# Scatters that add scored expert outputs to one total per token, in place of stored rows that are read back

## The chip, the cores and the metric

The kernel runs on one core of one Trainium2 chip. The metric is the device time of one execution in microseconds (us). A core has TensorE (PE in the profile; its weight loads are PEld), VectorE (DVE), ScalarE (ACT), GpSimd (POOL) and SyncE (SP), and 16 DMA engines that move data between the chip's memory and the on-chip SBUF. An engine's own instructions run in order; between engines, and between engines and DMAs, only semaphores hold an order.

## The reference

Two layers over 512 tokens of 1024 features: a Mamba-2 mixer and then a forgetting attention, each followed by a mixture of experts. What the change touches is the mixture of experts, which both layers have:

```python
scores = sigmoid(t @ w_router)                   # 512 x 64
eidx   = top 8 of (scores + bias), inside the 4 best of 8 groups
wsel   = scores at eidx / their sum * 2.5
out = (silu(t @ ws1) * (t @ ws3)) @ ws2          # shared expert
for each expert e:
    a = silu(t @ w1[e]) * (t @ w3[e])
    out += (a * gate[:, e]) @ w2[e]              # gate = wsel where chosen, else 0
x = layer_norm(alpha * x + (1 + gate2) * out)
```

Each token is sent to 8 of 64 experts, so an expert has 64 tokens on the mean (512 * 8 / 64). All is float32.

## The kernel before

All engines' programs are written out by hand, each with its semaphores; nothing is scheduled by a tool. Where several reads stand in one order, that is the order of the code.

**Before the experts.** The mixer's result, normalized, is written as rows to `rows_dram` (512 x 1024). DVE picks each token's 8 experts (`mask`), numbers the tokens of an expert (`pos`), and numbers the experts of a token from 0 to 7 (`krank`, a scan over the mask). PE multiplies a one-hot matrix of the places with `V` (token number times 8, and `krank`), which gives for each of an expert's 128 slots the row `8 * token + rank` that its output will have; a slot without a token gets a number past the end. DVE writes both this number and the token number (shifted by 3) to `table`.

**The expert loop.** 64 experts, in groups of 8 (`SLOTS`), `with ... Fori` over the groups in the middle. For each expert: SP loads w1, w3, w2 (three DMAs of 512 KB) as soon as its slot of eight is free, that is after the `down` product of the expert 8 earlier; POOL (`fetch`) gathers the expert's token rows with an indirect DMA into one of 4 tiles `xg`, five experts ahead; PE transposes them (L771), ACT copies and scales them (L1240), PE makes the two up products (L793), ACT and DVE the gated product, PE the down product (L805); DVE multiplies it with `g2bc` on its way into one of 4 tiles `yrow` (L1829); POOL (`send`, L2173) scatters `yrow` with an indirect DMA to the rows of `part_dram`, a tensor of 4096 rows with one row for each token and rank. Slots without a token have an index out of bounds, and nothing of them is moved. POOL's program is: fetch of expert i + 5, send of expert i, fetch of i + 6, and so on. A `carrier`, a tiny tensor operation (L2148), stands ahead of each indirect DMA and carries its waits. `yrow[u % 4]` may be written again once the scatter of four experts earlier has landed (`y_out`).

**After the loop.** SP reads `part_dram` back by rank: seven DMAs of 2 MB (`rank[k]`, L2428) and the last rank in four of 512 KB (L2432). No rank is complete before the last experts, as each of a token's ranks can be with almost any expert, so load k waits until expert 56 + k is scattered (`until_sent`). DVE multiplies ranks 0 to 2 with the token's gate and adds them to `SH`, which already holds the shared expert and the residual (`add_row`, L1800), partly between the steps of the last group of experts; the gates of each rank are worked out there too (`gates_whole`, `gates_of`, L1778 and L1782). Ranks 3 to 7 go through PE: ACT makes diagonal matrices of gates (`diagonal`, L1255), and PE multiplies each with its rows, 80 matmuls of 128x512 (L875) into all 8 PSUM banks. DVE adds the banks to `SH` (L1934) and normalizes tile by tile. In the first layer the first three weight blocks of the shared keys and values come next on SP; two of their buffers still hold ranks 5 and 6, so they wait for PE (`part_read`).

**Zeros.** Early in the program SP fills `part_dram` with zeros (four DMAs of 4 MB), which makes rows that nothing was scattered to harmless.

An expert with more than 128 tokens takes extra blocks (`more_blocks`, `over`); with these inputs none has, and those branches are not taken.

## Time and profile before

| | us |
|---|---|
| median of 3 runs | 2006.43 |
| lowest, highest | 1999.59, 2013.11 |
| the profiled execution | 2011.6 |
| its span (first to last instruction) | 2009.8 |
| PE busy in the span | 1848.4 (92%) |
| DVE busy | 907.5 (45%) |
| ACT busy | 742.4 (37%) |
| POOL busy | 649.9 (32%) |

The span lies 1.8 us under the profiled execution's time, and that execution 5.2 us above the median. A sum of differences made against the span can therefore be put onto the median unchanged. The page of the profile cuts the span into 40 slices of 50.2 us. The two expert loops lie in slices 14 to 22 and 31 to 40 (about 663 to 1089 us and 1520 to 1950 us). There the row of the DMA engines stands at 8 or 9 tenths and PE at 9.

In the rows below, a line of the timeline reads: start in us, duration in us, engine, line, operation, what it writes and reads, how many, and in brackets the idle time ahead of it with what ended it. SPq is SP's DMA queue: its duration there reaches from the first to the last issue of merged DMAs.

### The profile page before, as it was taken

How to read it: one execution, taken by the hardware profiler on the slowest of the kernel's cores; microseconds unless marked ns; L12 is line 12 of the kernel's file. 1: busy time of each engine (PE TensorE's matmuls, PEld its weight loads, DVE VectorE, ACT ScalarE, POOL GpSimd, SP SyncE). 2: the span in 40 equal slices, each digit the busy share in tenths (PEclk: the TensorE clock that was granted, in tenths of full speed). 3: DMA queues.
4: the chain of work that ended last, by engine and by line, in shares of the span. 5: the costliest groups of instructions: out<-in, count | busy, mean ns of one | idle time of the engine just before them, and what ended most of it. 6: DMA issues, size and time to landing. Idle time of an engine off the chain costs nothing. (4 is left out here: it accounts for less than half of the span.)

```text
span 2009.8 us, 29708 instructions
## 1 busy us (share of the span) xinstructions
PE 1848.4 (92%) x9848; PEld 1275.9 (63%) x9848; DVE 907.5 (45%) x2097; ACT 742.4 (37%) x1913; POOL 649.9 (32%) x796
## 2 busy tenths in 40 slices
PE   2999999988999899999997799999998999999976
PEld 2644444567444688888885346558656888888852
DVE  4677754377313533333345401237444333333453
ACT  2433310255112544444443200134245444444431
POOL 4143300055212474444442340000133744444421
PEclk9799999999999899999998899999998999999988
DMA  9475646491203799999988403200237898999883
GB/s 341 161 273 215 247 151 210 168 335 43 79 11 123 278 334 335 330 328 331 329 293 343 154 28 112 80 17 1 69 112 273 315 328 319 324 342 343 314 313 133
DMA packets 178546, 443.90 MB, mean 221 GB/s; under 512 B 36004, under 2 KB 43540, under 8 KB 178452
## 3 DMA queue, kind: packets, MB, share of 16 engines
q1 hardware_dynamic: 140436, 371.31, 51.6%
q0 software_dynamic: 38016, 71.39, 9.5%
q8 instruction: 53, 0.87, 0.2%
q14 instruction: 41, 0.34, 0.0%
HBM read 419.39 MB, written 90.23 MB: 254 GB/s over the span
## 5 line engine op out<-in xcount | busy, mean ns | idle before, releaser
L1240 ACT ACTIVATE arena<-psum,lncol 128x128 f32<-128x128 f32 x1024 | 371.5, 469 | 423.6 <-PE psum L771 397.4
L793 PE MATMUL psum<-arena 128*128 128x128 f32 x4096 | 501.9, 278 | 0.0
L793 PEld LDWEIGHTS psum<-arena 128*128 128x128 f32 x4096 | 479.2, 193 | 1.0 <-issue 1.0
L805 PE MATMUL psum<-arena 128*128 128x512 f32 x512 | 243.6, 598 | 9.3 <-DVE arena L1829 9.3
L1717 DVE TENSOR_REDUCE destf<-psum 128x3 f32 (+1 forms) x112 | 18.0, 161 | 416.7 <-PE psum L793 399.6
L2148 POOL TENSOR_TENSOR passed<-ones 128x1 f32<-128x1 f32 x256 | 61.1, 239 | 405.2 <-DVE arena L1829 393.8
L557 PE MATMUL psum<-arena 128*128 128x512 f32 x384 | 178.5, 627 | 0.0
L771 PEld LDWEIGHTS psum<-ident,arena 128*128 128x128 f32 x1024 | 123.6, 144 | 74.2 <-issue 65.4
L1829 DVE TENSOR_TENSOR arena<-psum,arena 128x512 f32<-128x512 f32 x256 | 165.7, 683 | 7.8 <-PE psum L805 5.9
L1385 DVE SCALAR_TENSOR_TENSOR arena<-arena,condT 128x512 f32<-128x512 f32 x126 | 150.7, 1196 | 11.7 <-DMA arena<-in_ada_w_dram 7.3
L2164 POOL DMA_INDIRECT arena<-h_rows,idx x128 | 140.5, 1098 | 22.8 <-issue 7.3
L771 PE MATMUL psum<-ident,arena 128*128 128x128 f32 x1024 | 138.5, 280 | 7.1 <-DMA arena<-h_rows,idx 5.0
L2173 POOL DMA_INDIRECT expert_rows<-arena,idx x128 | 131.2, 1025 | 27.2 <-issue 26.9
L2122 POOL DMA_DIRECT2D h_rows<-arena x8 | 4.9, 618 | 416.2 <-ACT arena L1070 416.2
L557 PEld LDWEIGHTS psum<-arena 128*128 128x128 f32 x384 | 76.7, 202 | 94.8 <-issue 94.8
L805 PEld LDWEIGHTS psum<-arena 128*128 128x128 f32 x512 | 88.0, 192 | 73.0 <-issue 71.7
L2073 POOL TENSOR_TENSOR arena<-arena 128x2048 f32<-128x2048 f32 (+1 forms) x20 | 73.1, 3657 | 162.4 <-ACT arena L1097 161.6
L571 PE MATMUL psum<-arena 128*128 128x512 f32 x256 | 111.8, 594 | 0.0
L702 PE MATMUL psum<-arena 128*128 128x512 f32 x256 | 110.9, 592 | 0.0
L1710 DVE TENSOR_TENSOR arena<-slot_no,arena 128x512 bf16<-128x512 bf16 x128 | 87.2, 685 | 0.1
L702 PEld LDWEIGHTS psum<-arena 128*128 128x128 f32 x256 | 48.3, 190 | 58.7 <-issue 58.4
L571 PEld LDWEIGHTS psum<-arena 128*128 128x128 f32 x256 | 48.1, 190 | 57.9 <-issue 57.9
(265 smaller groups left out, 2364.6 us busy)
## 6 DMA issues: line engine op xcount, KB each, us to landing
arena<-in_moe_w_dram SPq DMA_DIRECT2D x384, 512.0 KB
arena<-in_ada_w_dram SPq DMA_DIRECT2D x32, 1024.0 KB, 5.2
arena<-expert_rows SPq DMA_DIRECT2D x14, 2048.0 KB, 13.3
arena<-in_ssm_w_in_dram SPq DMA_DIRECT2D x10, 2048.0 KB, 10.3
arena<-in_ada_w_dram SPq DMA_DIRECT2D x8, 2048.0 KB, 10.8
expert_rows<-arena SPq DMA_DIRECT2D x4, 4096.0 KB, 27.4
arena<-in_ssm_w_out_dram SPq DMA_DIRECT2D x4, 2048.0 KB, 9.4
arena<-in_kv_ada_w_dram SPq DMA_DIRECT2D x4, 1024.0 KB, 5.3
```

What stands on the lines that cost most here:

```text
L557: mm = pe.matmul(ps[:, :], w[:, k, P * j:P * j + P], HT[:, k, :], start=(k == 0), stop=(k == KC - 1))
L571: mm = pe.matmul(ps[:, :], HT[:, k, P * t:P * t + P], w[:, k, :], start=(k == 0), stop=(k == KC - 1))
L702: mm = pe.matmul(ps[:, :], xbcT[:, k, tok(t)], w_blocks[n][k // KC][:, k % KC, :], start=(k == 0), stop=(k == XT - 1))
L771: mm = pe.transpose(psum[:, b, P * j:P * j + P], xg[u % 4][:, P * k:P * k + P], ident[:, :])
L793: mm = pe.matmul(psum[:, b, 0:P], w[:, k, :], xeT[u % 2][:, k, :], start=(k == 0), stop=(k == KC - 1))
L805: mm = pe.matmul(psum[:, b, :], aT[u % 2], exp_w[u][:, 2, 512 * n:512 * n + 512], start=True, stop=True)
L1240: ins = act.activation(xeT[u % 2][:, k, :], psum[:, b, P * j:P * j + P], ACT.Identity, scale=h_scale(l, k), bias=h_shift(l, k))
L1385: ins = dve.scalar_tensor_tensor(ada_acc[0], ada_dve[:, k, :], condT[:, k:k + 1], ada_acc[0], ALU.mult, ALU.add)
L1710: dve.tensor_tensor(onehot[u % 4], slot_no[:, :].unsqueeze(1).to_broadcast([P, T, P]), pos[:, :, one].to_broadcast([P, T, P]), ALU.is_equa ...
L1829: dve.tensor_tensor(yrow[u % YROWS][:, cols_], psum[:, b, :], g2bc[:, cols_], ALU.mult).then_inc(drained[b], 1)
L2164: pool.indirect_dma_start(out=xg[u % 4], out_offset=None, in_=rows_dram, in_offset=bass.IndirectOffsetOnAxis(ap=idx[u][:, 1:2], axis=0), b ...
L2173: pool.indirect_dma_start(out=part_dram, out_offset=bass.IndirectOffsetOnAxis(ap=idx[u][:, 0:1], axis=0), in_=yrow[u % YROWS], in_offset=None,
```

## The change

- `part_dram` (4096 rows, one per token and rank) goes. In its place stands one tensor of 512 rows per layer (`sum_dram[l][a]`, with `SUMS = 1`), one row for each token. Each scatter adds its rows to what is there (`compute_op=ALU.add`).
- Two scatters that add to one row must not overlap in time, so `send` waits until the scatter before it has landed.
- The row index is now the token number itself, so `krank` and the shift by 3 go, and `table` and `idx` have one column.
- The score of a token for its expert has to be with the slot. POOL splits the scores into three bfloat16 parts (`split_scores`), which are columns 2 to 4 of `V`; the one-hot product, now with 5 columns and not 3, brings them to the slots; DVE adds them up (`gslot`), copies one expert's column to `gnow`, and multiplies it into the output in the instruction that empties PSUM. The division by the sum of a token's scores is done at the end with `gsum`.
- After the loop SP reads one total, four tiles of 512 KB, and DVE does one multiply-add per tile (`add_sums`). The eight rank loads, the gates by rank, the diagonals and the 80 matmuls go.
- Zeros are written for two tensors of 2 MB instead of 16 MB.

```diff
-DVE_ROWS = 3
-NOWHERE = 2 * S * TOPK
+SUMS = 1
+NOWHERE = 2 * S
...
-        part_dram = nc.dram_tensor("expert_rows", [S * TOPK, D], F32, kind="Internal").ap()
+        sum_dram = [[nc.dram_tensor(f"expert_sum{l}{a}", [S, D], F32, kind="Internal").ap() for a in range(SUMS)]
+                    for l in range(2)]
...
                             for t in range(T):
-                                pe.matmul(psum[:, b, P:P + 3], onehot[u % 4][:, t, :],
+                                pe.matmul(psum[:, b, P:P + 5], onehot[u % 4][:, t, :],
...
-                for b in range(8):
-                    claim(b)
-                for k in range(DVE_ROWS, TOPK):
-                    pe.wait_ge(gdiag_ready, (TOPK - DVE_ROWS) * l + k - DVE_ROWS + 1)
-                    if k < TOPK - 1:
-                        pe.wait_ge(part_in[k], 16 * (l + 1))
-                    for t in range(T):
-                        if k == TOPK - 1:
-                            pe.wait_ge(last_part_in[t], 16 * (l + 1))
-                        for n in range(2):
-                            mm = pe.matmul(psum[:, 2 * t + n, :], gdiag[T * (k - DVE_ROWS) + t],
-                                           rank[k][:, t, 512 * n:512 * n + 512],
-                                           start=(k == DVE_ROWS), stop=(k == TOPK - 1))
...
                 def write_table(e, ps):
...
+                    dve.tensor_scalar(table[:, one], ps[:, P:P + 1], ps[:, P + 1:P + 2], float(NOWHERE), ALU.add,
+                                             ALU.add).then_inc(table_ready, 1)
+                    return dve.tensor_reduce(gslot[:, one], ps[:, P + 2:P + 5].rearrange("p (e c) -> p e c", c=3), AX, ALU.add)
...
+                    dve.tensor_copy(gnow[:, u:u + 1], gslot[:, one]).then_inc(gate_ready, 1)
...
-                        dve.tensor_tensor(yrow[u % YROWS][:, cols_], psum[:, b, :], g2bc[:, cols_], ALU.mult
-                                          ).then_inc(drained[b], 1)
+                        dve.scalar_tensor_tensor(yrow[u % YROWS][:, cols_], psum[:, b, :], gnow[:, u:u + 1], g2bc[:, cols_],
+                                                 ALU.mult, ALU.mult).then_inc(drained[b], 1)
...
+                def add_sums(a, t):
+                    dve.wait_ge(part_in[a][t], 16 * (l + 1))
+                    return dve.scalar_tensor_tensor(SH[:, t, :], part[a][:, t, :], gsum[:, t:t + 1], SH[:, t, :],
+                                                    ALU.mult, ALU.add)
...
                 for t in range(T):
-                    for n in range(2):
-                        r = SH[:, t, 512 * n:512 * n + 512]
-                        ps = until_filled(dve, ("parts", l, t, n))
-                        dve.tensor_tensor(r, ps, r, ALU.add).then_inc(drained[MARK[("parts", l, t, n)][0]], 1)
...
+                    step(add_sums(SUMS - 1, t))
...
+            def split_scores(l, t0, t1):
+
+                R = slice(t0, t1)
+                pool.wait_ge(sig_ready, T * l + t1)
+                step(pool.tensor_copy(V[:, R, :, 2], scores[:, R, :]))
+                settle()
+                step(pool.tensor_tensor(rest[:, R, :], scores[:, R, :], V[:, R, :, 2], ALU.subtract))
+                settle()
+                step(pool.tensor_copy(V[:, R, :, 3], rest[:, R, :]))
+                settle()
+                pool.tensor_tensor(V[:, R, :, 4], rest[:, R, :], V[:, R, :, 3], ALU.subtract).then_inc(split_ready, 1)
...
                 def send(g, u):
 
                     for b in (3, 7):
                         pool.wait_ge(drained[b], base[b] + SLOTS * g + u + 1)
+                    if u >= SUMS or l or not isinstance(g, int) or g:
+                        v = (u - SUMS) % SLOTS
+                        pool.wait_ge(y_out[v % YROWS], 16 * (2 * g + (v // YROWS + 1 if u >= SUMS else 0))
+                                     + 16 * (E // YROWS) * l)
                     carrier(u)
-                    pool.indirect_dma_start(out=part_dram,
+                    pool.indirect_dma_start(out=sum_dram[l][u % SUMS],
                                             out_offset=bass.IndirectOffsetOnAxis(ap=idx[u][:, 0:1], axis=0),
                                             in_=yrow[u % YROWS], in_offset=None,
-                                            bounds_check=last_part, oob_is_err=False).then_inc(y_out[u % YROWS], 16)
+                                            bounds_check=last_row, oob_is_err=False, compute_op=ALU.add).then_inc(y_out[u % YROWS], 16)
...
-                rows_of = part_dram.rearrange("(t p k) d -> k p t d", p=P, k=TOPK)
-                for k in range(TOPK - 1):
-                    until_sent(sp_, l, E - TOPK + k)
...
-                    sp_.dma_start(rank[k], rows_of[k]).then_inc(part_in[k], 16)
-                when_more(sp_, l, more_blocks, over)
-                until_sent(sp_, l, E - 1)
-                for t in range(T):
-                    sp_.dma_start(rank[TOPK - 1][:, t, :], rows_of[TOPK - 1, :, t, :]).then_inc(last_part_in[t], 16)
+                for a in range(SUMS):
+                    if a == SUMS - 1:
+                        when_more(sp_, l, more_blocks)
+                    until_sent(sp_, l, E - SUMS + a)
                     for t in range(T):
+                        sp_.dma_start(part[a][:, t, :], sum_dram[l][a][TILES[t], :]).then_inc(part_in[a][t], 16)
```

POOL's program inside the loop of the middle groups, before, from one send to the next. `passed` is the carrier's tile; `drained3` and `drained7` say that DVE has emptied the two banks of the down product.

```order
196 L2148 TENSOR_TENSOR passed<-ones 128x1 [waits drained7]
197 L2173 DMA expert_rows<-arena,idx 4096x1024
198 L2157 REGISTER_ALU [waits y_out3]
199 L2158 REGISTER_ALU [waits filled4]
200 L2159 ISA [waits table_ready]
201 L2159 COPY idx<-arena 128x2
202 L2148 TENSOR_TENSOR passed<-ones 128x1 [waits idx_ready]
203 L2164 DMA arena<-h_rows,idx 128x1024
204 L2171 REGISTER_ALU
205 L2171 REGISTER_ALU [waits drained3]
206 L2148 TENSOR_TENSOR passed<-ones 128x1 [waits drained7]
207 L2173 DMA expert_rows<-arena,idx 4096x1024
```

The same place now:

```order
195 L2066 DMA expert_sum<-arena,idx 512x1024
196 L2046 REGISTER_ALU [waits y_out2]
197 L2047 REGISTER_ALU [waits filled4]
198 L2048 ISA [waits table_ready]
199 L2048 COPY idx<-arena 128x1
200 L2037 TENSOR_TENSOR passed<-ones 128x1 [waits idx_ready]
201 L2053 DMA arena<-h_rows,idx 128x1024
202 L2060 REGISTER_ALU
203 L2060 REGISTER_ALU [waits drained3]
204 L2063 ISA [waits drained7]
205 L2037 TENSOR_TENSOR passed<-ones 128x1 [waits y_out0]
206 L2066 DMA expert_sum<-arena,idx 512x1024
```

The instructions and their order are the same; the carrier ahead of the scatter has a further wait, for the landing of the scatter that POOL issued just before (`y_out0` here). The gather of the next expert stands between the two scatters as it did.

SP's program from the last part of the first layer's experts to the weights of the keys and values, before:

```order
199 L2432 DMA arena<-expert_rows 128x1024 [waits y_out2,y_out3,y_out1,y_out0]
200 L2432 DMA arena<-expert_rows 128x1024 x3
201 L2325 DMA arena<-in_ln_g_dram 128x1024
202 L2326 DMA arena<-in_ln_b_dram 128x1024
203 L2302 DMA arena<-in_kv_w_dram 128x8x512
204 L2302 DMA arena<-in_kv_w_dram 128x8x512 [waits part_read]
```

And now:

```order
189 L2309 DMA arena<-expert_sum 128x1024 [waits y_out2,y_out3,y_out1,y_out0]
190 L2309 DMA arena<-expert_sum 128x1024 x3
191 L2218 DMA arena<-in_ln_g_dram 128x1024
192 L2219 DMA arena<-in_ln_b_dram 128x1024
193 L2195 DMA arena<-in_kv_w_dram 128x8x512 x2
```

The seven rank loads ahead of this place are gone, and the second weight block no longer waits for PE to have read a rank.

## Rows read from the trace of the kernel before

**Rows 1.** Stretches inside the two expert loops: each engine's busy time.

```profile
core 0: us, PE busy (x) PEld busy (x) DVE busy (x) ACT busy (x) POOL busy (x), PEclk, DMA share, GB/s
690.00:890.00 200.00, 200.00 (x1512) 167.75 (x1509) 77.88 (x222) 96.10 (x283) 104.39 (x167) 1.00 0.92 329
1560.00:1900.00 340.00, 340.00 (x2570) 285.77 (x2569) 136.01 (x391) 164.90 (x484) 158.70 (x275) 1.00 0.92 330
```

**Rows 2.** Timeline of POOL, two experts of the steady loop.

```profile
746.16 1.01 POOL L2173 DMA_INDIRECT expert_rows<-arena,idx  x1 [0.16 <-issue]
...
747.80 1.05 POOL L2164 DMA_INDIRECT arena<-h_rows,idx  x1
752.22 0.18 POOL L2148 TENSOR_TENSOR passed<-ones 128x1 f32<-128x1 f32 x1 [3.37 <-DVE arena L1829]
752.56 1.02 POOL L2173 DMA_INDIRECT expert_rows<-arena,idx  x1 [0.16 <-issue]
...
758.86 1.01 POOL L2173 DMA_INDIRECT expert_rows<-arena,idx  x1 [0.16 <-issue]
```

**Rows 3.** Timeline at the first layer's loop end: POOL's last nine scatters, in part.

```profile
1044.20 1.02 POOL L2173 DMA_INDIRECT expert_rows<-arena,idx  x1 [0.44 <-issue]
...
1081.28 1.00 POOL L2173 DMA_INDIRECT expert_rows<-arena,idx  x1 [0.15 <-issue]
1085.33 1.09 POOL L2148 TENSOR_TENSOR passed<-ones 128x1 f32<-128x1 f32 x1 [3.05 <-DVE arena L1829]
1086.57 0.99 POOL L2173 DMA_INDIRECT expert_rows<-arena,idx  x1 [0.15 <-issue]
1087.72 1.09 POOL L2148 TENSOR_TENSOR passed<-ones 128x1 f32<-128x1 f32 x1 [0.16 <-DVE arena L1829]
1088.96 1.86 POOL L2173 DMA_INDIRECT expert_rows<-arena,idx  x1 [0.15 <-issue]
```

**Rows 4.** Timeline there: what waited for landings, on ACT and SP.

```profile
1089.40 1.28 ACT L1255 ACTIVATE arena<-ident,gk 128x128 f32<-128x128 f32 x4 [7.31 <-DMA expert_rows<-arena,idx]
...
1093.07 0.36 SPq L2428 DMA_DIRECT2D arena<-expert_rows  x1
1098.71 1.77 SPq L2432 DMA_DIRECT2D arena<-expert_rows  x4
```

**Rows 5.** Timeline at the first loop's start: first gather, first transposes.

```profile
663.48 1.56 POOL L2164 DMA_INDIRECT arena<-h_rows,idx  x1 [0.16 <-issue]
...
671.52 1.97 PE L771 MATMUL psum<-ident,arena 128*128 128x128 f32 x8 [2.56 <-DMA arena<-h_rows,idx]
```

**Rows 6.** Page, part 6: DMA issues, KB each, median us to landing.

```profile
h_rows<-arena POOLq DMA_DIRECT2D x8, 512.0 KB, 3.0
```

**Rows 7.** Page, part 3: DMA queues.

```profile
q1 hardware_dynamic: 140436, 371.31, 51.6%
q0 software_dynamic: 38016, 71.39, 9.5%
```

**Rows 8.** Timeline of SP: when expert weights stop being issued.

```profile
1036.66 2.13 SPq L2375 DMA_DIRECT2D arena<-in_moe_w_dram  x2
1038.88 1.78 SPq L2378 DMA_DIRECT2D arena<-in_moe_w_dram  x1
1051.22 42.21 SPq L2428 DMA_DIRECT2D arena<-expert_rows  x7
```

**Rows 9.** Timelines of PE and DVE after the first loop.

```profile
1092.71 36.98 PE L875 MATMUL psum<-arena 128*128 128x512 f32 x80 [6.03 <-issue]
...
1123.72 0.69 DVE L1934 TENSOR_TENSOR arena<-psum,arena 128x512 f32<-128x512 f32 x1 [31.37 <-PE psum L875]
1124.57 0.69 DVE L1934 TENSOR_TENSOR arena<-psum,arena 128x512 f32<-128x512 f32 x1 [0.17 <-PE psum L875]
```

**Rows 10.** Timelines of POOL and DVE after the second loop.

```profile
1949.50 1.86 POOL L2173 DMA_INDIRECT expert_rows<-arena,idx  x1 [0.15 <-issue]
...
1984.63 0.69 DVE L1934 TENSOR_TENSOR arena<-psum,arena 128x512 f32<-128x512 f32 x1 [0.17 <-PE psum L875]
```

**Rows 11.** Timelines: stalls inside the last group, DVE and PE.

```profile
1067.01 1.28 DVE L1800 SCALAR_TENSOR_TENSOR arena<-arena,gk 128x1024 f32<-128x1024 f32 x1 [7.20 <-DMA arena<-expert_rows]
...
1069.04 2.56 PE L805 MATMUL psum<-arena 128*128 128x512 f32 x4 [3.45 <-DVE arena L1829]
1928.72 3.75 PE L805 MATMUL psum<-arena 128*128 128x512 f32 x4 [4.64 <-DVE arena L1829]
```

**Rows 12.** Groups of instructions by line: DVE's multiplies out of PSUM.

```profile
L1829 DVE TENSOR_TENSOR arena<-psum,arena 128x512 f32<-128x512 f32 x256 | 165.7, 683 | 7.8 <-PE psum L805 5.9 <-issue 0.4
L1614 DVE SCALAR_TENSOR_TENSOR arena<-psum,rsy,arena 128x512 f32<-128x512 f32 x8 | 6.0, 750 | 79.0 <-PE psum L702 79.0
```

More of the change, by code:

```diff
@@ L153, in trunk @@
         yrow = [view(16 + 4 * i, D) for i in range(YROWS)]
-        RANK_HOME = (0, 95, 111, 127, 0, 143, 159, 32)
-        rank = [view(kb, T, D) for kb in RANK_HOME]
-        RANK_IN_RING = {0: 1, 1: 2}
-        gdiag = [view(kb + 0.5 * i, P) for kb, n in ((92, 6), (69, 6), (90.5, 3), (73, 1), (20, 4)) for i in range(n)]
-        gate_main = view(64, T, E)
         zero = view(141, 512)
-        part_over = view(95, TOPK, D)
+        part = [view(95 + 16 * a, T, D) for a in range(SUMS)]
         lnrow_moe = [view(80, D), view(84, D)]
-        scores, sel, mask, gate, krank = (view(64 + i, T, E) for i in range(5))
+        scores, sel, mask = (view(64 + i, T, E) for i in range(3))
+        rest = view(67, T, E)
         top8 = view(70, T * EG, 8)
@@ L211, in trunk @@
         grank = sb("grank", [P, T, EG])
-        gk = sb("gk", [P, T, TOPK])
-        gk_over = gsc
         gsum = sb("gsum", [P, T])
-        V = sb("V", [P, T, E, 3], BF16)
-        destf = sb("destf", [P, E])
-        table = view(90, E, 2).bitcast(I32)
+        V = sb("V", [P, T, E, 5], BF16)
+        gslot = view(68, E)
+        gnow = view(68.5, SLOTS + 1)
+        table = view(90, E).bitcast(I32)
         pos1 = view(74.75, T)
-        V1 = view_b(74.5, T, 4)
-        idx = [sb(f"idx{i}", [P, 2], I32) for i in range(8)]
+        V1 = view_b(74.5, T, 8)
+        idx = [sb(f"idx{i}", [P, 1], I32) for i in range(8)]
         passed = sb("passed", [P, SLOTS + 3])
@@ L310, in trunk @@
             "onehot", "dest", "idx", "rows", "turned", "moved", "weights", "up", "silu", "gated", "down", "yrow",
-            "sent", "step", "carried", "over_in", "over_step", "over_added")} for l in range(2)]
+            "sent", "step", "carried")} for l in range(2)]
         idx_ready = sem("idx_ready")
@@ L372, in when_more @@
                     blocks(stage)
-                with eng.Else():
-                    eng.nop()
-            if over is not None:
-                key = eng.value_load(more_keyi[0:1, 0:1])
-                with eng.If(key > OVER):
-                    over()
                 with eng.Else():
@@ L836, in unit @@
                         for t in range(T):
-                            mm = pe.matmul(psum[:, 6, 0:3], onehot[0][:, t, :], V1[:, t, 0:3], start=(t == 0), stop=(t == T - 1))
+                            mm = pe.matmul(psum[:, 6, 0:5], onehot[0][:, t, :], V1[:, t, 0:5], start=(t == 0), stop=(t == T - 1))
                         mm.then_inc(done["dest"], 1)
@@ L1262, in group @@
                         silu(g, u)
-                        if last and u > DVE_ROWS:
-                            diagonal(u - 1)
                 rows_in(0, 0)
@@ L1685, in route @@
                     ins.then_inc(mask_ready, 1)
-                for t in ts:
-                    ins = dve.tensor_tensor_scan(krank[:, t, :], mask[:, t, :], mask[:, t, :], 0.0, ALU.add, ALU.bypass)
-                step(ins)
-                settle()
-                step(dve.tensor_tensor(krank[:, R, :], krank[:, R, :], mask[:, R, :], ALU.subtract))
-                settle()
-                step(dve.tensor_copy(V[:, R, :, 2], krank[:, R, :]))
-                settle()
             mixed(0)
@@ L1847, in group @@
                             rows_out(g - 1, SLOTS - 1)
-                        if last and u >= SLOTS // 2:
-                            add_row(2 * u - SLOTS + 1)
                 group(0, first=True)
@@ L1930, in experts @@
                 for t in range(T):
-                    for n in range(2):
-                        r = SH[:, t, 512 * n:512 * n + 512]
-                        ps = until_filled(dve, ("parts", l, t, n))
-                        dve.tensor_tensor(r, ps, r, ALU.add).then_inc(drained[MARK[("parts", l, t, n)][0]], 1)
-                    for n in range(2):
-                        until_drained(dve, ("parts", l, t, n))
+                    step(add_sums(SUMS - 1, t))
                     statistics(k, t, SH)
```

181 lines of the change are left out of this document (43 added, 138 removed).

## The prediction

> **What bounds the kernel now.** I read the stretches by engine first, then POOL's timeline inside a loop, then both loop ends, and last the page's parts on DMA.
>
> In both expert loops PE is busy for the whole of the stretch at full granted clock [rows 1]. An expert takes what lies between two scatters, here 6.40 and 6.30 us, 6.35 us over the two (758.86 - 746.16 = 12.70) [rows 2]. Two loops of 64 experts are some 810 us of the 2010. PE sets the pace, but with little to spare behind it: the 16 DMA engines are busy for 0.92 of the same stretches [rows 1]. So the loop is bound by PE with DMA at 92% of a second bound. POOL is idle for 3.37 us of each expert, waiting for DVE [rows 2].
>
> After each loop there is a tail that no expert work covers. In the first layer the last scatter is issued at 1088.96 [rows 3], SP issues the last rank's loads at 1098.71 [rows 4], PE spends 36.98 us on the rank products, and DVE has the first tile complete at 1124.57 + 0.69 = 1125.26 [rows 9]. In the second layer: 1949.50 to 1984.63 + 0.69 = 1985.32 [rows 10]. That is 36.3 and 35.8 us.
>
> **What the change takes away.** The new tail: last scatter issued, its landing R, SP's first load of 512 KB, one DVE multiply-add of 1024 columns. A transfer of 512 KB between SBUF and memory takes 3.0 us from issue to landing with little beside it [rows 6]; the multiply-add takes 1.28 us, as L1800 has the same form [rows 11]; 0.4 us goes for the issue [rows 4]. R is not in the trace without other traffic. Bounds: 3.0 us [rows 6], and 8.1 us (below). No weights move then, so I take 5. Tail = 5 + 0.4 + 3.0 + 1.3 = 9.7 us. Gain: 26.6 and 26.1, together 52.7 us. The later tiles keep their pace, since the normalization's steps on DVE, ACT and POOL are not touched.
>
> Inside the last group DVE now stands 7.20 us for rank 0's load, and PE behind it 3.45 us, in the second layer 4.64 us [rows 11]. Both go: 8.1 us. Against this, the last two scatters were issued 2.4 us apart [rows 3] and may no longer overlap: the last one starts at 1086.57 + 5 + 0.3 instead of 1088.96, 2.9 us later, 6 us for both layers. Together the change saves 52.7 + 8.1 - 6 = **55 us**.
>
> Edits at nothing: 12 MB less of zeros, written early in the program, when no expert needs the memory; the 5-column one-hot product, a few columns in a matmul; DVE's work per expert, where one small instruction of the table goes and one copy comes, and the two multiplies out of PSUM cost 750 ns, not 683 [rows 12], 0.13 us more. DVE is busy for 78 of 200 us [rows 1], so this hides behind PE; laid bare it would be 0.13 * 128 = 17 us. `split_scores` is eight small POOL operations that run while DVE picks experts. `krank`'s steps go from DVE there, under 1 us. The keys' weights start earlier too, but PE waits for the normalized tiles at that point, not for them.
>
> **What the change adds: one wait per expert.** A scatter may be issued only when the one before has landed. Behind POOL's waiting carrier stand the scatter itself and the next gather. For the scatter waits the `yrow` tile (four of them), so DVE stops after four experts, then PE's down product, then all of PE. The gathers are five ahead and are not late first. Hence in the steady loop one expert takes the larger of 6.35 us and c = R + 0.34, where R is issue to landing under load and 0.34 is carrier to issue (752.22 to 752.56) [rows 2]. No loss as long as R is under 6.0 us.
>
> What is R under load? For a plain scatter: the one issued at 1081.28 [rows 3] held ACT until 1089.40 [rows 4], 8.1 us. The one issued at 1086.57 released SP's load at 1093.07, 6.5 us at most. The one issued at 1088.96 released SP at 1098.71, at most 9.7 us. A first gather, of as many rows as a scatter, took 671.52 - 663.48 = 8.0 us beside the first weights [rows 5]. At the other end stands 3.0 us for the undisturbed 512 KB [rows 6]. So c lies between 6.35 (R below 6.0) and 8.1 + 0.34 = 8.5 us, if adding costs nothing, and the four loaded rows are all above 6.0.
>
> Two things push R apart. A slower loop thins the weights: at 8 us an expert they are there for a fifth less of the time, and the gather before has mostly left the queue. That takes R down. The add takes it up: the destination has to be read as well. The software queue has 9.5% of 16 engines' span [rows 7], which is 191 us in two loops for gathers and scatters, so 95 us for scatters. If an adding packet takes twice a plain one, the DMA share in the loops goes from 0.92 by 95 / 810 = 0.12 to 1.04, above what there is: even a perfectly spread load makes an expert 6.35 * 1.04 = 6.6 us.
>
> For weights and scatters together I take c = 8.0 us: near the 8.1 of the nearest row, as the same instruction with as many rows under load, with the thinner load and the dearer packet about cancelling.
>
> What a page says of the add: the Trainium skill ("Collectives: The Full Stack", The bandwidth ceiling) states that a reduction in the DMA engines is half as fast as a copy, because each chunk has two source reads on one ring. No row here shows it. The Trainium skill's "DMA: Bandwidth & Descriptors" (The descriptor swizzle) puts partitions 0 to 63 on engines 0 to 7; the mean expert fills 64 slots, so half the engines would carry nearly all scattered rows, and the mean share of 0.92 would hide an almost full half. By both rules together an estimate is 7.6 us an expert from bandwidth alone, and the sum would end near 2090 us.
>
> How many experts pay: the loss needs weights in flight. SP issues the last weights at 1038.88 + 1.78, and nine of the layer's 64 scatters are issued after that, from 1044.20 to 1088.96 [rows 3, 8]; beside those only rank loads move now, which go. That leaves 55 scatters a layer, 110 in all. Loss: 110 * (8.0 - 6.35) = **182 us**. The later ones land in less than PE's pace.
>
> **Sum.** -55 + 182 = +127 us on a span of 2009.8; on the median of 2006.43 this is **2133 us**. The range of c for this case is 7.0 to 9.7 us, as the landings in the rows run from 6.5 to 9.7 us less what a thinner load gives and plus what the add costs: 2023 to 2320 us.
>
> **Rivals.**
> 1. *The landing hides (faster).* If a scatter under a steady loop lands within 6.0 us, nothing in the loop moves and only the savings remain: 2006 - 55 = 1951 us; with c at 6.5, 110 * 0.15 = 17 more, 1968. For it: those landings of 8 us were measured beside 2 MB loads or the burst of first weights, and POOL's 3.37 us of idle time say that a gather is out 4.4 us ahead of its scatter. Against it: DMA at 0.92. It decides at R = 6.0 us.
> 2. *Only bandwidth counts.* The wait hides, but the add's reads fill the DMA engines: c = 6.6, 2006 - 55 + 28 = 1979 us.
> 3. *The add is slow by itself.* If each adding packet waits for its read before the next goes, R is a sum of round trips; with R above 10 us an expert costs 10.5 and more: 2006 - 55 + 110 * 4.15 = 2408 us and up. Nothing in the trace speaks for or against it.
>
> **How the numbers follow.** Forecast 0.60; rival 1 0.21; rival 2 0.07; rival 3 0.12. A measurement of this kernel, whose three runs spread over 0.7%, tells about 1% from no change. Slower by over 1% (above 2026.5): nearly all of the forecast and rival 3, 0.71. Within 1%: 0.06, from the ends of the forecast and of rival 2. Faster: 0.23. The range leaves out rival 3 and a part of rival 1's and the forecast's ends: 1951 to 2320 us; cases of both signs are in it, and the likeliest one's own range is 2023 to 2320.
>
> **What would show it.** In the changed profile: the distance of two scatters in the loop (forecast 8.0, rival 1 6.35 to 6.5); POOL's carrier L2037 waiting for the DMA of the scatter and not for DVE; PE idle at the down product behind DVE; PE's busy share of the loop falling from 1.00 to about 0.8, which can also cost granted clock; the weight queue less dense. Each tail from last scatter to first added tile at about 10 us. The prediction is wrong if the carrier still waits for DVE, or if the scatter distance is above 10.

## The result and the profile after

The changed kernel takes **2278.57 us** (median of 4 runs, 2266.93 to 2290.34) where the kernel before took 2009.77 (1999.59 to 2017.87) beside it: a ratio of 1.134 with a 95% interval of 1.126 to 1.142. That is 269 us more; 127 were forecast. The two profiled executions have spans of 2009.8 and 2265.1 us, 255.3 apart, and the accounts below are made on these.

The stretches in the first loop, of after, with the columns of [rows 1]:

```profile
690.00:890.00 200.00, 171.13 (x1172) 141.17 (x1171) 74.79 (x175) 75.20 (x219) 97.16 (x122) 0.93 0.81 257
890.00:1060.00 170.00, 133.23 (x908) 110.47 (x909) 46.91 (x127) 59.01 (x171) 63.92 (x95) 0.92 0.73 231
```

PE stood at 200.00 of 200 before [rows 1]; now it is busy for 86% and then 78% of the time, at a granted clock of 0.93 and 0.92 of its upper level. The matmul count says it better than the busy time, as matmuls at a lower clock are busy for longer: 1172 where there were 1512. The DMA engines move 257 and 231 GB/s in place of 329, weights for the most part.

What the engines wait for, over the whole span, of after (line waited for: us in total, times, longest):

```profile
POOL passed L2037 <- DMA expert_sum<-arena,idx: 561.5, 122, 7.5
PE psum L759 <- DMA arena<-h_rows,idx: 197.9, 86, 5.6
POOL passed L2037 <- DVE arena L1733: 32.9, 5, 10.1
```

The first line is the wait that was added. Before, POOL's carrier waited for DVE [rows 2]; now it waits for the landing of the previous scatter in 122 of 128 experts. The second line was not foreseen: PE waits for gathers.

Two experts of the steady loop, POOL's timeline of after, to be read beside [rows 2]:

```profile
803.07 1.60 POOL L2066 DMA_INDIRECT expert_sum<-arena,idx  x1 [0.16 <-issue]
804.12 0.75 POOL L2048 COPY idx<-arena 128x1 int32 x1
804.96 0.19 POOL L2037 TENSOR_TENSOR passed<-ones 128x1 f32<-128x1 f32 x1
805.29 1.06 POOL L2053 DMA_INDIRECT arena<-h_rows,idx  x1
811.89 0.18 POOL L2037 TENSOR_TENSOR passed<-ones 128x1 f32<-128x1 f32 x1 [5.53 <-DMA expert_sum<-arena,idx]
812.55 1.60 POOL L2066 DMA_INDIRECT expert_sum<-arena,idx  x1 [0.48 <-issue]
```

A scatter issued at 803.07 releases the carrier at 811.89: a landing of 8.8 us under load. The next one goes at 812.55. So one cycle here is 8.8 + 0.66 = 9.5 us, where it was 6.3 to 6.4 [rows 2]. While weights move the cycles run from 6.4 to 11.5 us. Their mean is 9.0 and 9.1 us in the two layers: 54 cycles in 485.2 us and 55 in 498.4.

The end of the first loop, POOL's timeline of after:

```profile
1208.74 1.57 POOL L2066 DMA_INDIRECT expert_sum<-arena,idx  x1 [0.47 <-issue]
1215.25 0.18 POOL L2037 TENSOR_TENSOR passed<-ones 128x1 f32<-128x1 f32 x1 [4.93 <-DMA expert_sum<-arena,idx]
...
1235.16 1.56 POOL L2066 DMA_INDIRECT expert_sum<-arena,idx  x1 [0.44 <-issue]
```

No weights move here (42 GB/s in all from 1208 to 1216). The landing is 6.5 us even so, and the last nine cycles are 6.8 us on the mean.

Behind it, the tail on SP's queue, DVE and POOL, of after:

```profile
1241.32 1.76 SPq L2309 DMA_DIRECT2D arena<-expert_sum  x4
...
1244.82 1.28 DVE L1795 SCALAR_TENSOR_TENSOR arena<-arena,gsum 128x1024 f32<-128x1024 f32 x1 [27.96 <-DMA arena<-expert_sum]
...
1253.34 2.33 POOL L1987 TENSOR_TENSOR arena<-arena 128x1024 f32<-128x1024 f32 x1 [16.61 <-DVE arena L1810]
...
1253.49 3.27 DVE L1795 SCALAR_TENSOR_TENSOR arena<-arena,gsum 128x1024 f32<-128x1024 f32 x1
...
1259.88 3.27 DVE L1795 SCALAR_TENSOR_TENSOR arena<-arena,gsum 128x1024 f32<-128x1024 f32 x1
```

From the last scatter to the first added tile: 1235.16 to 1244.82 + 1.28 = 1246.10, 10.9 us where it was 36.3 [rows 3, 9]. In the second layer it is 10.6 us where it was 35.8 [rows 10]. The same multiply-add takes 1.28 us alone and 3.27 us when POOL's own 128x1024 addition has just begun.

**Where the time went.** First to last scatter of a loop, before and after, and the rest:

| | before | after | difference |
|---|---|---|---|
| layer 1, first to last scatter | 399.9 | 546.3 | +146.4 |
| layer 2, first to last scatter | 401.9 | 552.8 | +150.9 |
| tails, to the first added tile | 36.3, 35.8 | 10.9, 10.6 | -50.6 |
| all the rest, by subtraction: the tiles behind it in both layers above all | | | about +9 |
| span | 2009.8 | 2265.1 | +255.3 |

So the savings came as forecast, and the loops lost 297 us. The question for the experiments is what makes the cycle 9.0 us: the wait, the add, or what the DMA engines have to carry.

### The profile page after: what moved, and what is told of

Read it like the earlier page. It is cut to its first block, busy times and chain, and to the rows that moved or that the text cites. A ratio compares the mean times of both kernels' runs of the same rounds, so it can differ in the third digit from the quotient of the medians.

```text
span 2265.1 us, 29193 instructions
## 1 busy us (share of the span) xinstructions
PE 1855.6 (82%) x9688; PEld 1296.7 (57%) x9688; DVE 891.6 (39%) x2009; ACT 734.0 (32%) x1873; POOL 735.5 (32%) x812
## 3 DMA queue, kind: packets, MB, share of 16 engines
q0 software_dynamic: 38016, 71.42, 13.4%
## 4 chain that ended last, share of the span: by engine, by line
PE 38%; DMA 37%; issue 9%; POOL 7%; DVE 7%; ACT 2%; POOLq 1%; SPq 0%; DVEq 0%; ACTq 0%
DMA expert_sum<-arena,idx 34%; PE psum L557 5%; PE psum L688 5%; PE psum L543 5%; PE psum L871 3%; PE psum L885 2%; PE psum L912 2%; DVE arena L1344 2%; PE psum L781 2%; DMA arena<-h_rows,idx 2%; PE psum L982 2%; PE psum L951 2%; PE psum L929 2%; POOL expert_sum L2066 1%; PE psum L658 1%
## 5 line engine op out<-in xcount | busy, mean ns | idle before, releaser
L781 PE MATMUL psum<-arena 128*128 128x128 f32 x4096 | 548.2, 294 | 0.0
L759 PE MATMUL psum<-ident,arena 128*128 128x128 f32 x1024 | 163.8, 312 | 198.0 <-DMA arena<-h_rows,idx 197.9
L1715 DVE COPY arena<-arena 128x1 f32 (+1 forms) x128 | 19.7, 154 | 749.2 <-PE psum L781 722.6
L759 PEld LDWEIGHTS psum<-ident,arena 128*128 128x128 f32 x1024 | 132.3, 159 | 289.9 <-issue 199.8
L2037 POOL TENSOR_TENSOR passed<-ones 128x1 f32<-128x1 f32 x256 | 54.1, 211 | 605.3 <-DMA expert_sum<-arena,idx 561.5
L2066 POOL DMA_INDIRECT expert_sum<-arena,idx x128 | 207.8, 1623 | 53.1 <-issue 49.7
L1733 DVE SCALAR_TENSOR_TENSOR arena<-psum,arena 128x512 f32<-128x512 f32 x256 | 182.1, 744 | 14.6 <-PE psum L793 13.9
L2048 POOL COPY idx<-arena 128x1 int32 (+1 forms) x128 | 98.0, 765 | 19.1 <-DVE arena L1667 14.2
L1661 DVE TENSOR_TENSOR arena<-slot_no,arena 128x512 bf16<-128x512 bf16 x128 | 102.7, 806 | 0.1
## 6 DMA issues: line engine op xcount, KB each, us to landing
arena<-in_kv_ada_w_dram SPq DMA_DIRECT2D x2, 2048.0 KB, 10.6
```

The costliest lines, as they stand in the source:

```text
L759: mm = pe.transpose(psum[:, b, P * j:P * j + P], xg[u % 4][:, P * k:P * k + P], ident[:, :])
L781: mm = pe.matmul(psum[:, b, 0:P], w[:, k, :], xeT[u % 2][:, k, :], start=(k == 0), stop=(k == KC - 1))
L1661: dve.tensor_tensor(onehot[u % 4], slot_no[:, :].unsqueeze(1).to_broadcast([P, T, P]), pos[:, :, one].to_broadcast([P, T, P]), ALU.is_equa ...
L1733: dve.scalar_tensor_tensor(yrow[u % YROWS][:, cols_], psum[:, b, :], gnow[:, u:u + 1], g2bc[:, cols_], ALU.mult, ALU.mult).then_inc(draine ...
L2066: pool.indirect_dma_start(out=sum_dram[l][u % SUMS], out_offset=bass.IndirectOffsetOnAxis(ap=idx[u][:, 0:1], axis=0), in_=yrow[u % YROWS], ...
```

## The experiments

The theories that are left at the end: the wait counts, with a landing that the add lengthens (A in the expectations); the DMA engines have too much to carry in sum (C); half of them have too much, as the rows lie in half of the partitions (D; no trace here names the engine of a packet, so "half of the engines" is the theory's word and what is tested is the half of the partitions). Any other letter is explained by the numbers given with it, and the runs bore none of them out. Each kernel is the changed one with the edit shown, unless it says otherwise. All ratios are to the kernel before, run beside it.

### The add taken out, the wait left

```diff
-    bounds_check=last_row, oob_is_err=False, compute_op=ALU.add).then_inc(y_out[u % YROWS], 16)
+    bounds_check=last_row, oob_is_err=False).then_inc(y_out[u % YROWS], 16)
```

> The changed kernel with the add taken out of the scatters: each scatter writes its rows over what is there, so of a token's eight contributions only the last remains, and the output is wrong by that. The wait for the scatter before stays. Theory A (the add makes each landing longer, and the wait turns landings into the loop's pace): the distance of two scatters in the loop falls from the 9.1 us of the changed kernel to 6.5 to 7.5, and the undisturbed scatters at a loop's end, 6 to 7 us apart, come to 4 to 5; total 2020 to 2090 us. Theory B (the landing is long by the weights beside it, the add is free): the distance stays near 9, total near 2270 us.

Measured: 2039.17 us, ratio 1.014 (1.002 to 1.026). Its loop end on POOL's timeline, without weights beside it:

```profile
1091.72 1.01 POOL L2066 DMA_INDIRECT expert_sum<-arena,idx  x1 [0.49 <-PE psum L759]
1095.14 0.18 POOL L2037 TENSOR_TENSOR passed<-ones 128x1 f32<-128x1 f32 x1 [0.73 <-DMA expert_sum<-arena,idx]
1095.81 1.00 POOL L2066 DMA_INDIRECT expert_sum<-arena,idx  x1 [0.49 <-issue]
```

A plain scatter lands in 3.4 us there, with a gather still beside it, an adding one in 6.5 with none. POOL's own part grows as well: issuing takes 1.0 us plain and 1.6 us adding. The mean cycle over a whole loop falls from 8.7 and 8.8 to 6.9 and 7.1 us, and that of the steady part from 9.0 to 7.3. The queue of gathers and scatters, from the part on DMA queues of the page, first of after, then of this kernel:

```profile
q0 software_dynamic: 38016, 71.42, 13.4%
```

```profile
q0 software_dynamic: 38016, 71.39, 9.8%
```

The packets and bytes are the same. 13.4% of 2265.1 us is 303 us of 16 engines; 9.8% of 2046.2 is 200 us. The add alone costs 103 us of them. In a plain kernel about half of the queue's 200 us are scatters, so an adding packet occupies its engine for about twice as long. The Trainium skill's "Collectives: The Full Stack" (The bandwidth ceiling) has a reduction between cores half as fast as a copy, by a second read for each chunk. The queue here fits that factor: 103 us more on some 100 us of scatters. That it is the second read that takes the time is not shown by any run.

### Two and four totals, so that a scatter waits for an older one

```diff
-SUMS = 1
+SUMS = 2
-        part = [view(95 + 16 * a, T, D) for a in range(SUMS)]
+        part = [view((95, 111, 127, 32)[a], T, D) for a in range(SUMS)]
...
                     for t in range(T):
                         step(add_sums(a, t))
+                    settle()
```

With four totals the first line is `SUMS = 4`.

> The changed kernel with two totals in place of one (even experts add to one, odd ones to the other), so a scatter waits for the landing of the one two before. The adds stay as they are; one more 2 MB of total is read and added at the end. Theory A (the wait is the bound): two landings of 9 us share 2 cycles, so the wait asks for 4.5 us an expert and PE's 6.35 bounds again: total 1955 to 1990 us. Theory C (the adds' traffic is the bound, the wait only shows it): the distance stays at 7.6 us or more, total 2090 us or more.

> The changed kernel with four totals: a scatter waits for the one four before, which DVE's use of the output tile asks for anyway, so no wait is added. Adds as they are. Theory A: 6.35 us an expert, total 1960 to 2000 us (the tail reads 8 MB in place of 2). Theory C (traffic): as with two totals, 7.6 us or more an expert, 2100 us or more.

Measured: 2078.16 us (1.033, 1.027 to 1.040) and 2082.06 us (1.035, 1.028 to 1.042). Both fall between the theories: A expected 1955 to 1990 and 1960 to 2000, C 2090 and 2100 or more, so each missed, A by 88 and 82 us, C by 12 and 18. Going from one total to two gives back 200 us, so the wait matters; a third and fourth give nothing, so from two on the wait is no longer what limits (with four, POOL's carrier waits 199.9 us of the first loop for DVE, and for a scatter hardly at all). Something else does. The kernel with four totals, the stretch (columns as in [rows 1]) and PE's timeline:

```profile
690.00:890.00 200.00, 189.51 (x1392) 158.89 (x1391) 88.00 (x202) 89.33 (x261) 116.39 (x156) 0.97 0.90 285
```

```profile
802.87 2.05 PE L781 MATMUL psum<-arena 128*128 128x128 f32 x16 [2.11 <-DMA arena<-in_moe_w_dram]
...
813.10 3.78 PE L781 MATMUL psum<-arena 128*128 128x128 f32 x16 [3.61 <-DMA arena<-in_moe_w_dram]
```

PE waits for expert weights, which it did not do before. The DMA engines are busy for 0.90 of the stretch on the mean, close to the 0.92 of before [rows 1], but what they move falls from 329 to 285 GB/s. Most cycles are 6 to 7 us, and from about the twentieth expert on every fifth or so is 8 to 13 us, as if the lead in weights had first to be used up; the mean is 7.1. PE's idle time is 5% of the stretch, and its granted clock of 0.97 in place of 1.00 takes another 3%: together the 8% of matmuls that are missing (1392 for 1508 in the next kernel). So a part of this price is PE's clock after its waits. That weights come late at a mean share of 0.90 speaks for a bandwidth limit that the mean does not show; where it lies is tested below.

### The same four totals without the add

This is the previous kernel with the edit of the first, so neither an add nor a wait that binds.

> Four totals and no add in the scatters (rows are overwritten, so most of a token's contributions are lost and the output is wrong by that). No added wait, no added traffic: what the change saves alone. All theories: 6.35 us an expert as in the kernel before, two tails of 10 to 20 us in place of 36, total 1955 to 1975 us. Beside the run with four totals and adds it gives the price of the adds' traffic alone.

Measured: 1977.96 us (0.983, 0.978 to 0.989), 3 us above the range expected. Its stretch:

```profile
690.00:890.00 200.00, 200.00 (x1508) 167.62 (x1507) 80.64 (x222) 95.63 (x282) 103.07 (x163) 1.00 0.90 322
```

PE has its 200 of 200 us back, and the mean cycle is 6.26 us. With this the four corners stand. From 1978 us, the wait alone adds 61 us, the add alone 104, and both together 301. The two together cost far more than 61 + 104: the add lengthens just what the wait waits for (a landing of 6.5 us against 3.4, above). (The two corners with four totals also read 16 tiles back behind a loop and not 4, so their tails are longer; the 61 and 104 are right to some ten us at best.)

### The rows spread over all partitions

A mean expert has 64 tokens in 128 slots, and they filled slots 0 to 63, one per partition. The edit numbers the slots 0, 2, 4, ... 126, 1, 3, ..., so that token rows lie in partitions of both halves:

```diff
-            pool.iota(slot_no[:, :], [[1, P]], base=0, channel_multiplier=0,
+            pool.iota(slot_no[:, :], [[1, 2], [2, P // 2]], base=0, channel_multiplier=0,
-                    step(dve.tensor_scalar(load_expert, load_expert, P - 1, None, ALU.bitwise_and))
+                    step(dve.tensor_scalar(load_expert, load_expert, P - 1, 1, ALU.bitwise_and, ALU.logical_shift_right))
```

The second line undoes the doubling where the same numbers count experts. First with one total, wait and add, as in the changed kernel:

> The changed kernel (one total, wait and add as they are) with the slots in another order: places 0, 2, 4 and so on stand in partitions 0 to 63, places 1, 3, 5 in 64 to 127, so an expert's 64 or so rows use both halves of the partitions and not only the lower. Theory D (the moved rows lie on half of the DMA engines, and these are the full ones): landings get shorter by about half of what the rows take, the undisturbed ones at a loop's end from 6.1 to about 4.5 us, the loaded ones from 9 to 6.5 to 7; total 2040 to 2110 us. Theory E (the rows are spread already, or an add costs a fixed time whatever the engine): no difference, 2278 us within 1%.

Measured: 2141.67 us (1.064, 1.057 to 1.070). 137 us less than the changed kernel, by the place of the rows alone; the range expected, 2040 to 2110, was missed by 32. Its loop end on POOL's timeline:

```profile
1149.22 1.56 POOL L2066 DMA_INDIRECT expert_sum<-arena,idx  x1 [0.44 <-issue]
1154.26 0.18 POOL L2037 TENSOR_TENSOR passed<-ones 128x1 f32<-128x1 f32 x1 [3.47 <-DMA expert_sum<-arena,idx]
1154.88 1.56 POOL L2066 DMA_INDIRECT expert_sum<-arena,idx  x1 [0.44 <-issue]
1161.23 0.18 POOL L2037 TENSOR_TENSOR passed<-ones 128x1 f32<-128x1 f32 x1 [4.79 <-DMA expert_sum<-arena,idx]
```

The first of these landings without weights is 5.0 us, where the same expert's was 6.4 in the changed kernel, but the second is 6.4 us, where it was 6.3. So the gain differs from expert to expert; the mean of the last nine cycles goes from 6.8 to 6.0 us. With weights moving the mean cycle is 7.8 and 8.0 us in place of 9.0 and 9.1, and over a whole loop 7.6 and 7.8: the wait is still what binds.

Then with two totals:

> Two totals and the slots spread over both halves. Theory D: with two totals PE waited for expert weights in every few experts, since the engines with the rows were full; spread, they are not, an expert costs 6.35 us again, and the total is 1955 to 1980 us, below the kernel before. Theory E: as with two totals alone, 2078 us.

Measured: 1970.69 us (0.979, 0.975 to 0.983). The stretch, and POOL's timeline:

```profile
690.00:890.00 200.00, 200.00 (x1518) 168.34 (x1518) 93.31 (x218) 96.89 (x285) 126.30 (x167) 1.00 1.01 330
```

```profile
753.04 0.18 POOL L2038 TENSOR_TENSOR passed<-ones 128x1 f32<-128x1 f32 x1 [2.42 <-DVE arena L1733]
753.70 1.60 POOL L2067 DMA_INDIRECT expert_sum<-arena,idx  x1 [0.48 <-issue]
```

The total is in the range that D expected, 1955 to 1980. PE is busy throughout, 330 GB/s are moved (329 before [rows 1]), the mean DMA share is 1.01, above the 0.90 at which weights came late, and POOL waits for DVE again, for 2.42 us. The adds are all still there: q0 takes 14.9% of this kernel's 1966.5 us, 293 us. So it was not the sum of the DMA work that was too much (C), but that the rows lay in half of the partitions (D). Against two totals without spreading it is 107 us.

That adding rows in half of the partitions load half of the engines is what the Trainium skill's "DMA: Bandwidth & Descriptors" (The descriptor swizzle) would have: it puts partitions 0 to 63 on engines 0 to 7, for a transfer of 1 MiB to 128 partitions. The runs agree by the 285 and 330 GB/s above. They do not show which engine carries which row, so another thing that the two halves of the partitions do not share would fit them as well. The edit also moves the gathered rows, not only the added ones; their part was not measured apart.

### The spreading and the plain kernels

Does spreading help where nothing is added? First the kernel with the wait and without the add, then the kernel before, each with the edit of spreading alone:

> One total, wait kept, add taken out (rows overwritten, so most of a token's contributions are lost and the output is wrong by that), slots spread over both halves. Theory A with D (the loop's pace is the landing, made of the rows per engine and of the add): loaded landings come under 6.0 us, the wait hides, an expert costs 6.35 to 6.7 us; total 1950 to 1990 us. If it stays near the 2039 us of the same kernel with slots not spread, the landing of a plain scatter does not depend on how many engines carry it, and the spread acts on adds alone.

> The kernel before with nothing changed but the order of the slots (an expert's rows in both halves of the partitions). If PE bounds its loops, as the profile says, shorter landings bring nothing there: same time within 1%, 2000 to 2020 us, at most a few us less at the two loop ends, where the last scatters are waited for. If its loops were secretly held by the full half of the DMA engines, it gets faster by more than 1%, below 1990 us, and part of what the kernels with spread slots gained belongs to that and not to the change.

Measured: 1987.70 us (0.988, 0.982 to 0.993), 51 us less than without spreading; and 1994.77 us (0.990, 0.987 to 0.994). The first fell within its range, though the wait does not hide whole: POOL's carrier still waits for a scatter 56 times in the first loop, and the cycles while weights move are 6.8 and 6.7 us. For the second the cycle in the loop stays at 6.3 us on the mean, as expected, with its 200 of 200 us on PE. What it gains lies mostly in the last group. DVE's timeline of that kernel, to be read beside [rows 11]:

```profile
1064.50 1.28 DVE L1800 SCALAR_TENSOR_TENSOR arena<-arena,gk 128x1024 f32<-128x1024 f32 x1
```

It no longer stands there for 7.20 us waiting for rank 0. From first to last scatter the two loops are 5.3 and 7.4 us shorter (394.6 and 394.5 for 399.9 and 401.9), which is 12.7 of the 13.6 us between the two profiled spans, 2009.8 and 1996.2. The expectation was no change beyond 1%, 2000 to 2020 us; the ratio lies at that edge and the time 5 us below it. So some 19 us, or 1.0%, of what the spread kernels gain on the kernel before belongs to the spreading and not to the change: against this kernel the one with two totals and spreading (0.979) is 1.1% faster, not 2.1%.

The spread kernels also show the two causes apart: the wait alone 1987.70 us, the add alone (two totals) 1970.69, both together 2141.67. Each alone lies near the 1977.96 of the plain four totals (the corner with neither was not run with spread rows); the 150 us and more on top need a landing that is both waited for and longer.

### The tiles added first, normalized afterwards

On top of two totals and spreading: DVE adds all four tiles of the last total, then runs the normalization, in place of tile by tile.

```diff
                 for t in range(T):
                     step(add_sums(SUMS - 1, t))
+                for t in range(T):
```

> As the kernel with two totals and spread slots, but at the end DVE adds the total to all four tiles first and then normalizes tile by tile. In the changed kernel the third and fourth multiply-add of 1024 columns take 3.27 us and not 1.28, each beside POOL's add of the same width. If DVE and POOL hinder each other there, all four take 1.28 us now, the tiles' distance goes from 6.4 back to about 4.5 us, and each layer's end is 2 us shorter (two times 1.99 gained twice, less the first tile's later start): 0 to 6 us less than the other. If the 3.27 us come from something else, 2 to 4 us more.

Measured: 1964.49 us (0.976, 0.972 to 0.980), 6.2 us under the kernel with two totals and spreading, where 0 to 6 were expected. The intervals of the two ratios overlap, so it is the timelines that carry this. DVE and POOL behind the second loop:

```profile
1935.02 4.87 DVE L1795 SCALAR_TENSOR_TENSOR arena<-arena,gsum 128x1024 f32<-128x1024 f32 x4 [1.57 <-issue]
```

```profile
1948.70 2.35 POOL L1989 TENSOR_TENSOR arena<-arena 128x1024 f32<-128x1024 f32 x1 [1.17 <-DVE arena L1811]
1952.22 2.34 POOL L1989 TENSOR_TENSOR arena<-arena 128x1024 f32<-128x1024 f32 x1 [1.17 <-DVE arena L1811]
```

Four multiply-adds take 4.87 us, 1.2 each, now that none lies beside POOL's addition. The tiles follow at 3.5 us, with the additions done ahead of them, where the first three came 6.4 us apart with an addition between them in the changed kernel and in the one with two totals and spreading. This is the fastest version found: 2.4% under the kernel before, 1.0% of it by the spreading alone, with one total per token and layer replaced by two.

All of it in one table, in us:

| kernel | median | ratio | what limits the loop |
|---|---|---|---|
| changed (wait, add) | 2278.57 | 1.134 | wait on an adding scatter |
| wait, plain | 2039.17 | 1.014 | wait on a plain scatter |
| add, 2 totals | 2078.16 | 1.033 | weights that come late (rows in half of the partitions) |
| add, 4 totals | 2082.06 | 1.035 | the same |
| plain, 4 totals | 1977.96 | 0.983 | PE |
| spread, wait, add | 2141.67 | 1.064 | wait |
| spread, add, 2 totals | 1970.69 | 0.979 | PE |
| the same, tiles added first | 1964.49 | 0.976 | PE |
| spread, wait, plain | 1987.70 | 0.988 | PE for the most part, the wait in some experts |
| before, spread | 1994.77 | 0.990 | PE |

## Why the prediction was wrong in size

The direction and the mechanism were right: slower, by the one added wait, on POOL's carrier, with PE's share and granted clock falling. The size was off by 128 us on the span, +127 against +255.3. By the terms of the prediction's own sum:

| term | forecast | measured | off by |
|---|---|---|---|
| the loss of the experts that pay | 110 x 1.65 = +182 | 109 cycles, 983.6 us for 692.2 at 6.35: +291 | +109 |
| ends of the loops: stalls gone, last scatters serial | -8 + 6 = -2 | +6 | +8 |
| tails | -53 | -51 | +2 |
| the other tiles, with the remainder | 0 | +9 | +9 |
| sum | +127 | +255 | +128 |

**The step that failed is "I take c = 8.0 us".** The steady cycle was 9.0. The value was anchored to the 8.1 us of the nearest row, a plain scatter, "with the thinner load and the dearer packet about cancelling". They do not cancel. The runs give both parts. A plain scatter behind the wait makes steady cycles of 7.3 us, below the 8.1 + 0.34 that its nearest row gave; the add takes it from there to 9.0. ("The four loaded rows are all above 6.0" reads too much into them: two of the four, "6.5 us at most" and "at most 9.7", are upper bounds.) The undisturbed landing says the same without any load: 3.4 us plain, 6.5 adding. The prediction had noted that half of the engines might carry nearly all rows and that 0.92 would then hide an almost full half, but kept it out of the sum. With the rows spread, 137 of the 269 us went; with two totals as well, all of them. The prediction's 7.6 us an expert from bandwidth alone comes without its working; bandwidth without a wait that binds is the kernel with four totals, at 7.1.

**A smaller part of the same term** is "c = R + 0.34". From the carrier to the scatter it is now 811.89 to 812.55, with 0.48 us of it idle ahead of the issue, where 0.16 stood before [rows 2]; so it was R + 0.66. That is 0.3 of the 1.0 us by which c was off, some 35 of the 109 us. It comes neither from the add nor from which wait ends last, as the plain kernel (1095.14 to 1095.81) and the one in which POOL waits for DVE (753.04 to 753.70) have it too; why the idle time grew is open. The likeliest case's own range for c, 7.0 to 9.7, held the 9.0.

**"No weights move then, so I take 5."** The undisturbed landing was 6.5 us, and this has two effects. "The later ones land in less than PE's pace" fell: 6.5 + 0.6 is above 6.35, so the last 17 cycles of the two loops took 6.8 us each, and the stall that went was paid back by them (+6 in place of -2). The tails came out at 10.9 and 10.6 us for 9.7, which accounts for the 2 us.

**"The gathers are five ahead and are not late first."** They are late: PE waits 197.9 us for them and 0.2 us of the first loop at the down product, where it was looked for. PE's timeline of after:

```profile
803.39 1.19 PE L759 MATMUL psum<-ident,arena 128*128 128x128 f32 x8 [2.17 <-DMA arena<-h_rows,idx]
804.37 3.53 PE L781 MATMUL psum<-arena 128*128 128x128 f32 x16
...
807.84 2.03 PE L781 MATMUL psum<-arena 128*128 128x128 f32 x16
...
823.03 1.96 PE L759 MATMUL psum<-ident,arena 128*128 128x128 f32 x8 [3.98 <-DMA arena<-h_rows,idx]
```

The gather for expert i + 5 stands on POOL behind scatter i. Once POOL is what is late, "five ahead" is counted from POOL and not from PE, and PE uses up the lead. POOL would limit the loop with either, so by this argument, which no run tests, it changes where the idle time is seen and not how much there is.

**"The later tiles keep their pace, since the normalization's steps on DVE, ACT and POOL are not touched."** The steps are not, but their neighbour is. Before, DVE added the tiles out of PSUM; now the multiply-add reads and writes SBUF with 1024 columns while POOL's addition runs, and takes 3.27 us instead of 1.28. This is so for the third and the fourth tile of each layer; the first two, with no POOL addition beside them, take 1.28. The tiles come 6.4 us apart (1253.49 to 1259.88) and not 4.5. DVE's timeline of before, where each pair of additions out of PSUM took 1.28 us:

```profile
1127.67 1.28 DVE L1934 TENSOR_TENSOR arena<-psum,arena 128x512 f32<-128x512 f32 x2
...
1132.15 1.28 DVE L1934 TENSOR_TENSOR arena<-psum,arena 128x512 f32<-128x512 f32 x2
```

The last kernel, in which this meeting is avoided, takes 1.2 us for each addition.

**What held.** The gain of both tails to within 1.2 us each; the stalls in the last group gone; the added DVE work (0.13 us an expert) hidden; the zeros and the gates at nothing. Of the rivals, 1 and 2 were excluded by the 561.5 us of waiting, but what they describe is what two totals and spreading give: 1971 us measured, with 1951 to 1979 worked out for them. Rival 3, an add slow by itself with R above 10, was not it: with the same adds and no wait that binds, the loop runs at PE's pace.

What stays open: how much of the 9.0 us is time in the queue behind the weights and how much is the row's own read and write. Without weights the adding cycle is 6.8 us already and the plain one 4.1 (1091.72 to 1095.81); with weights they are 9.0 and 7.3. So the weights add 2.2 us to the one and 3.2 to the other, and the two parts do not simply add up.

## What to carry to other kernels

When a change makes each DMA wait for the one before, its cost is landing time under load minus what the slack covers, and the add must be priced in that landing: here about twice the time on the engine for each packet, and 3 us more even with no weights beside it. Two destinations, used in turn, took the wait away whole where four did no better. And look at which partitions the rows lie in: here weights came late at a mean DMA share of 0.90 with the rows in half of the partitions, and in time at 1.01 with the rows in both. Spreading them paid a little (1%) even where nothing was added.

## What the runs showed of the hardware that was not expected

- An adding scatter of about 64 rows of 4 KB landed in 6.5 us with no weights moving, a plain one in 3.4. Spread over both halves of the partitions one adding scatter's landing fell from 6.4 to 5.0, but the next one's did not (6.3 and 6.4).
- The issue of an adding scatter occupied POOL for 1.6 us and not 1.0, and the small copy behind it (L2048) took 0.75 us and not 0.20, partly during the issue.
- A DVE multiply-add of 128x1024 float32 in SBUF took 3.27 us when it ran beside a POOL addition of that size (2.33 us), and 1.28 us alone, a difference of almost the whole POOL operation.
- The granted clock of PE was 0.93 and 0.92 in stretches where PE was idle for 14% and 22% of the time, in gaps of some us between experts, and 1.00 in every loop in which it never waited. So a part of its time comes at the lower of the two levels, 1.2 GHz: the first up product behind the gap before 803.39 took 3.53 us, the next 2.03 us, with 16 matmuls in each, and the granted clock from 804.40 to 807.80 is 0.52. PE had been idle for 2.17 us just before, ahead of the transposes at 803.39. In the changed kernel, where POOL sets the pace, what this costs was not measured apart.
